# Two recurrence heads at a time: interleaved levels and pairwise tails in a hybrid decoder layer

## What is computed

```
b = jnp.cumsum(gc, axis=2)
diff = jnp.where(causal, b[:, :, :, None, :] - b[:, :, None, :, :], -jnp.inf)
att = jnp.einsum('bhtk,bhsk,bhtsk->bhts', qc, kc, jnp.exp(diff))
out = jnp.einsum('bhtk,bhkv->bhtv', qc * jnp.exp(b), S) + jnp.einsum('bhts,bhsv->bhtv', att, vc)
S = jnp.exp(b_last[:, :, 0, :])[..., None] * S + jnp.einsum('bhsk,bhsv->bhkv', kc * jnp.exp(b_last - b), vc)
```

## Time and profile before

| | |
|---|---|
| median of three runs | 1977.64 us (1977.2 to 1979.1) |
| profiled execution | 1976.55 us |
| its span | 1974.6 us |
| TensorE busy, share of the span | 1724.5 us, 87% |
| VectorE busy | 803.4 us, 41% |
| ScalarE busy | 432.9 us, 22% |
| GpSimd busy | 542.7 us, 27% |
| mean granted TensorE clock | 0.918 |

### The profile page before, as it was taken

The page is one execution under the profiler, slowest core; times in us unless marked ns, Lnnn a source line. Parts: engine busy times, 40 slices in busy tenths (PEclk is TensorE's granted clock), DMA queues, the critical chain, the costliest instruction groups (busy, mean ns, idle before and its releaser), DMA issues.

```text
span 1974.6 us, 28840 instructions
## 1 busy us (share of the span) xinstructions
PE 1724.5 (87%) x12863; PEld 1577.7 (80%) x12863; DVE 803.4 (41%) x1160; ACT 432.9 (22%) x576; POOL 542.7 (27%) x202
## 2 busy tenths in 40 slices
PE   2899999998797799877599978776688899999997
PEld 1799999998765799866388755554687899999997
DVE  4412111135217599866576654221465412111121
ACT  2311111112133123200123333221122211111111
POOL 0233343334312123300011122332122233333331
PEclk9999999999688899966599989887799999999999
DMA  4132233223311122201132137887512122333222
GB/s 136 43 86 73 74 101 86 79 69 117 121 48 34 55 89 86 75 23 44 51 115 67 68 126 284 316 303 299 207 64 86 49 80 73 89 90 82 79 74 78
DMA packets 191499, 203.43 MB, mean 103 GB/s; under 512 B 7104, under 2 KB 176832, under 8 KB 182928
## 3 DMA queue, kind: packets, MB, share of 16 engines
q1 hardware_dynamic: 172336, 105.56, 18.7%
q0 software_dynamic: 11680, 75.57, 10.5%
q10 hardware_dynamic: 7360, 20.47, 2.7%
HBM read 187.21 MB, written 14.30 MB: 102 GB/s over the span
## 4 chain that ended last, share of the span: by engine, by line
PE 75%; DVE 12%; DMA 6%; ACT 3%; issue 3%; SPq 0%; POOL 0%; ACTq 0%; DVEq 0%
PE ps L1291 21%; PE ps L1292 20%; PE ps L1293 20%; DMA k_page<-in_cache_k,kv_row 3%; DMA v_page<-in_cache_v,kv_row 2%; PE ps L1638 2%; PE ps L1591 1%; PE ps L1609 1%; DVE att L1033 1%; PE ps L1714 1%; DVE m_hi L1233 1%; DVE nf L841 1%; DVE n_lo L844 1%; ACT n_hi L515 1%; PE ps L1653 1%
## 5 line engine op out<-in xcount | busy, mean ns | idle before, releaser
L411 POOL TENSOR_TENSOR w_lo<-raw,w_hi 128x2048 fp32r<-128x2048 f32 (+1 forms) x108 | 456.7, 4229 | 1071.9 <-ACT w_hi L500 1071.9
L1291 PE MATMUL ps<-n_lo,w_hi 128*128 128x288 f32 x1856 | 557.6, 300 | 26.7 <-DVE n_lo L844 17.5
L1292 PE MATMUL ps<-n_hi,w_lo 128*128 128x288 f32 x1856 | 551.1, 297 | 0.0
L1293 PE MATMUL ps<-n_hi,w_hi 128*128 128x288 f32 x1856 | 549.3, 296 | 0.0
L1291 PEld LDWEIGHTS ps<-n_lo,w_hi 128*128 128x128 f32 x1856 | 351.6, 189 | 44.6 <-issue 28.7
L1293 PEld LDWEIGHTS ps<-n_hi,w_hi 128*128 128x128 f32 x1856 | 352.9, 190 | 0.0
L1292 PEld LDWEIGHTS ps<-n_hi,w_lo 128*128 128x128 f32 x1856 | 352.1, 190 | 0.0
L500 ACT ACTIVATE w_hi<-raw 128x2048 fp32r<-128x2048 f32 (+1 forms) x108 | 187.9, 1740 | 287.9 <-PE ps L1293 279.6
L856 DVE TENSOR_TENSOR hf<-sg,ps 128x576 f32<-128x576 f32 x44 | 33.2, 754 | 449.6 <-ACT sg L526 449.6
L1292 PE MATMUL ps<-hid_hi,w_lo 128*128 128x288 f32 x704 | 207.7, 295 | 0.0
L1293 PE MATMUL ps<-hid_hi,w_hi 128*128 128x288 f32 x704 | 207.5, 295 | 0.0
(11 more groups left out here) (256 smaller groups left out, 2317.1 us busy)
## 6 DMA issues: line engine op xcount, KB each, us to landing
raw<-in_w_in SPq DMA_DIRECT2D x23, 1024.0 KB, 5.3
raw<-in_ffn_w_gate SPq DMA_DIRECT2D x44, 512.0 KB, 4.0
raw<-in_ffn_w_up SPq DMA_DIRECT2D x44, 512.0 KB, 5.3
raw<-in_ffn_w_down SPq DMA_DIRECT2D x32, 704.0 KB, 4.5
scratch_g<-g_out ACTq DMA_DIRECT2D x8, 576.0 KB, 2.8
gates<-scratch_g ACTq DMA_DIRECT2D x4, 1152.0 KB, 8.8
raw<-in_w_out SPq DMA_DIRECT2D x4, 1024.0 KB, 4.9
scratch_x<-xT ACTq DMA_DIRECT2D x1, 2304.0 KB, 12.6
```

What stands on the lines that cost most here:

```text
L411: pool.tensor_tensor(w_lo[:, u % NRAW, :n], raw[:, u % NRAW, :n], w_hi[:, u % NW, :n].bitcast(F32), ALU.subtract).then_inc(S("w_lo_done"), 1)
L1291: pe.matmul(dst, hi, x_lo, start=first, stop=False)
L1292: pe.matmul(dst, lo, x_hi, start=False, stop=False)
L1293: return pe.matmul(dst, hi, x_hi, start=False, stop=last)
```

## The change

Heads are handled in groups of two, heads(g) for g = 0, 1. In the level loop each engine does level L of head a = 0, then of head a = 1, and goes on to the next level. Each head of the group has its own part of left, q_lev, k_lev, att, att_s, k_rows, state, state_s and v_own, and its own banks: 4 + a and 6 + a. There is one q_lev and k_lev buffer and one bank per head instead of two by level parity: VectorE waits for the products of level L-1 before it writes the operands of level L, and TensorE waits until level L-1 is copied out. The semaphores of the levels and the transfers exist once per a.

The tails follow pairwise: final operands of both heads, transposes of both, k_rows of both, v_own of both, then on TensorE the whole chain of the first head and that of the second; on VectorE the state updates of both, then state_s of both. The output of the second head goes to banks 4 and 6, and its v_own products to banks 2 and 3. TensorE waits for state_s_done and o_out once per group. GpSimd loads the states of two heads at the start, and each further one when the store of its buffer has landed. v_own moves to other memory, which is free there.

The lines that are removed stand in the functions above. The core of the diff:

```diff
@@ -248,15 +248,16 @@
         key, e = sb("key", [P, HB, T], at=e)
         query, e = sb("query", [P, HB, T], at=e)
         out_gate, e = sb("out_gate", [P, 4, T], at=e)
-        left, e = sb("left", [P, T], at=e)
+        left, e = sb("left", [P, 2, T], at=e)
         q_lev, e = sb("q_lev", [P, 2, T], at=e)
         k_lev, e = sb("k_lev", [P, 2, T], at=e)
-        att, e = sb("att", [P, 4, P], at=e)
-        att_s, e = sb("att_s", [NS, NS], at=e)
-        k_rows, e = sb("k_rows", [P, NT, KD], at=e)
-        state, e = sb("state", [P, 2, VD], at=e)
-        state_s, e = sb("state_s", [P, NB, VD], at=e)
-        v_own, e = sb("v_own", [NS, NB, VD], at=e)
+        att, e = sb("att", [P, 2, 4, P], at=e)
+        att_s, e = sb("att_s", [NS, 2, NS], at=e)
+        k_rows, e = sb("k_rows", [P, 2, NT, KD], at=e)
+        state, e = sb("state", [P, 2, 2, VD], at=e)
+        state_s, e = sb("state_s", [P, 2, NB, VD], at=e)
+        v_own, e = sb("v_own", [NS, 2, NB, VD], at=bias_at - 4 * (256 + 384 + 512))
+        assert e <= bias_p_at
 
...
+            def state_load(h):
+
+                if h < 2:
 
                     pool.wait_ge(S("index_done"), 1)
-                pool.dma_start(state_s[:, :, :], w["state_hgrn"][:, h].rearrange("b k v -> k b v")).then_inc(S("state_in"), 16)
+                else:
+                    pool.wait_ge(S(f"state_s_out{h % 2}"), 16)
+                pool.dma_start(state_s[:, h % 2, :, :], w["state_hgrn"][:, h].rearrange("b k v -> k b v")).then_inc(S(f"state_in{h % 2}"), 16)
+
+            def state_store(h):
                 pool.wait_ge(S("state_s_done"), h + 1)
-                pool.dma_start(out[9][0, :, h].rearrange("b k v -> k b v"), state_s[:, :, :]).then_inc(S("state_s_out"), 16)
-                pool.wait_ge(S("state_s_out"), 16 * (h + 1))
+                pool.dma_start(out[9][0, :, h].rearrange("b k v -> k b v"), state_s[:, h % 2, :, :]).then_inc(S(f"state_s_out{h % 2}"), 16)
 
...
+            state_load(0)
+            state_load(1)
+            for h in range(2):
+                state_store(h)
+                state_load(h + 2)
+            state_store(2)
+            state_store(3)
...
+            def heads(g):
+                for a in range(2):
+                    act.wait_ge(S("k_turned"), 2 * g + a + 1)
+                    act.activation(k_rows[:, a, 1:NT, :], ps[:, 4 + a, :].rearrange("p (t k) -> p t k", t=4), ACT.Copy)
+                    act.activation(k_rows[0:NS, a, 0, :], ps[0:NS, 6 + a, 0:KD], ACT.Copy).then_inc(S("k_rows_done"), 1)
+                for a in range(2):
+                    h = 2 * g + a
+                    act.wait_ge(S("o_summed"), h + 1)
+                    act.activation(oT[:, h, NS:T], ps[:, 4 * a, :], ACT.Copy)
+                    act.activation(oT[:, h, 0:NS], ps[:, 1 + 5 * a, 0:NS], ACT.Copy).then_inc(S("o_out"), 1)
+                    act.wait_ge(S("state_done"), 4 * h + 4)
+                    act.dma_start(out[5][0, 0, h], state[:, a, 1, :]).then_inc(S(f"state_out{a}"), 16)
...
+                    for a in range(2):
+                        h = 2 * g + a
+                        if L > 1:
+                            dve.wait_ge(S(f"level_done{a}"), 8 * g + L)
+                        dec, q, k = (level_view(x[:, h, :], L) for x in (decay, query, key))
+                        into_q, into_k = (level_view(x[:, a, :], L) for x in (q_lev, k_lev))
+                        dve.tensor_tensor(into_q[:, :, 1, :], q[:, :, 1, :], dec[:, :, 1, :], ALU.mult)
+                        if L == 1:
+                            dve.memset(left[:, a, :], 1.0)
+                            dve.tensor_copy(into_k[:, :, 0, :], k[:, :, 0, :]).then_inc(S(f"level_in{a}"), 1)
+                        else:
+                            dve.tensor_tensor(into_k[:, :, 0, :], k[:, :, 0, :], level_view(left[:, a, :], L)[:, :, 0, :],
+                                              ALU.mult).then_inc(S(f"level_in{a}"), 1)
+                        end, mid, first, right = level_views(h, L)
+                        dve.wait_ge(S(f"level_in{a}"), 8 * g + L)
+                        link(dve.tensor_tensor(first, first, end, ALU.mult))
+                        link(dve.tensor_tensor(right, right, mid, ALU.mult))
+                        level_out(a, L - 1)
+
+                for a in range(2):
+                    h = 2 * g + a
+                    dve.wait_ge(S(f"level_done{a}"), 8 * g + 8)
+                    dve.tensor_tensor(q_lev[:, a, :], query[:, h, :], decay[:, h, :], ALU.mult)
+                    dve.tensor_tensor(k_lev[:, a, :], key[:, h, :], left[:, a, :], ALU.mult).then_inc(S(f"level_in{a}"), 1)
+                    level_out(a, 7)
+                for a in range(2):
...
+                for a in range(2):
+                    h = 2 * g + a
+                    dec = decay[:, h, :]
+                    for i in range(4):
+                        dve.wait_ge(S("state_added"), 4 * h + i + 1)
...
+                for a in range(2):
+                    h = 2 * g + a
+                    dve.wait_ge(S("o_summed"), h + 1)
+                    link(dve.tensor_tensor(state_s[:, a, :, :], state_s[:, a, :, :],
+                                           decay[:, h, NQ - 1:NS:NQ].unsqueeze(2).to_broadcast([P, NB, VD]), ALU.mult))
+                    dve.wait_ge(S("head_read"), h + 1)
+                    for m in range(2):
+                        part = state_s[:, a, 4 * m:4 * m + 4, :]
+                        ins = dve.tensor_tensor(part, part, ps[:, 2 + m if a else 5 + 2 * m, :].rearrange("p (b v) -> p b v", b=4),
+                                                ALU.add)
+                    ins.then_inc(S("state_s_done"), 1)
...
+            def heads(g):
+                if g == 0:
...
+                    pe.wait_ge(S("o_out"), 2)
+                    pe.wait_ge(S("state_s_done"), 2)
                 for L in range(len(LEVELS)):
...
+                    for a in range(2):
+                        h = 2 * g + a
+                        if L:
+                            pe.wait_ge(S(f"level_in{a}"), 8 * g + L)
+                            pe.wait_ge(S(f"level_out{a}"), 8 * g + L)
+                        q = q_lev[:, a, :] if L else query[:, h, :]
+                        k = k_lev[:, a, :] if L else key[:, h, :]
+                        if LEVELS[L] < NQ:
+                            pe.matmul(ps[0:NS, 6 + a, 0:NS], k[:, 0:NS], q[:, 0:NS], start=True, stop=True)
+                        for t in range(1, NT):
+                            ins = pe.matmul(ps[:, 4 + a, P * (t - 1):P * t], k[:, cols(t)], q[:, cols(t)],
+                                            start=True, stop=True)
+                        ins.then_inc(S(f"level_done{a}"), 1)
+                for a in range(2):
+                    pe.wait_ge(S(f"level_in{a}"), 8 * g + 8)
+                    pe.wait_ge(S(f"level_out{a}"), 8 * g + 8)
+                    for t in range(NT):
+                        dst = ps[0:NS, 6 + a, 0:KD] if t == 0 else ps[:, 4 + a, P * (t - 1):P * t]
+                        ins = pe.transpose(dst, k_lev[:, a, cols(t)], ident)
+                    ins.then_inc(S("k_turned"), 1)
+                for a in range(2):
+                    h = 2 * g + a
+                    o_p, o_s = ps[:, 4 * a, :], ps[:, 1 + 5 * a, 0:NS]
+                    pe.wait_ge(S("k_rows_done"), h + 1)
+                    v = [stage[0:rows(t), g, t, a * VD:(a + 1) * VD] for t in range(NT)]
+                    for i in range(4):
+                        if 4 * h + i >= 2:
+                            pe.wait_ge(S("state_done"), 4 * h + i - 1)
+                        pe.matmul(ps[:, 2 + i % 2, 0:VD], k_rows[:, a, i + 1, :], v[i + 1], start=True,
+                                  stop=True).then_inc(S("state_added"), 1)
+                        pe.matmul(o_p[:, P * i:P * i + P], v[i + 1], att[:, a, i, :], start=True, stop=i == 0)
...
+                    pe.wait_ge(S("v_own_done"), h + 1)
+                    pe.wait_ge(S("k_rows_done"), 2 * g + 2)
+                    if a:
+                        pe.wait_ge(S("state_done"), 4 * h + 4)
+                    for m in range(2):
+                        ins = pe.matmul(ps[:, 2 + m if a else 5 + 2 * m, :], k_rows[0:NS, a, 0, :],
+                                        v_own[:, a, 4 * m:4 * m + 4, :], start=True, stop=True)
+                    ins.then_inc(S("head_read"), 1)
```

199 lines of the change are left out of this document (63 added, 136 removed).

## The result

| | before | after |
|---|---|---|
| median (range), runs of this comparison | 1978.37 us (1977.2 to 1980.81), 4 | 1961.07 us (1957.67 to 1964.96), 4 |
| ratio (95% interval) | | 0.9912 (0.989 to 0.9933) |
| profiled execution | 1976.55 us | 1957.67 us |
| its span | 1974.6 us | 1955.9 us |
| mean granted TensorE clock | 0.918 | 0.926 |

It is faster, by 17.3 us in the medians and 18.9 us in the two profiled executions. The forecast was 10.6 us less (1977.64 to 1967); 1961.07 lies inside the range of 1958 to 1974, near its low end.

What follows compares the result with a forecast made beforehand. VectorE was taken to bound the level loops, TensorE, with holes, the tails. Tail structure 9.1 us plus chains 2.9 less late groups 2.0 gave 10.0 us gained, so 1967 us; range 1958 to 1974.

Steps and rivals of the forecast that it cites:

- Tails' structure, 9.1 us: Tails: first head's transposes hidden, 2.8 us; k_rows copies hidden, 3.4 us; first head's state_s additions hidden, 2.9 us.
- the 2.9 us item: Tails: the first head's state_s additions run during the second head's chain; 1.45 us gone per pair, 2.9 us.
- Levels, 0 us of gain and 2.0 us of late groups: Level loops: VectorE sets the pace, so interleaving gains nothing; the tighter handshake with TensorE costs 1.0 us per pair.
- 0.15 us late at each of some five groups: Small levels at the low clock: TensorE's loop takes 2.73 us against VectorE's 2.58; 0.8 us per pair.
- 0.7 at the start of a pair: Pair start: TensorE runs three low-clock rounds, 7.5 us, before VectorE's third group, ready after two; 0.7 us more.
- Rival 4: Level loops: interleaving also fills VectorE's small gaps, 3.6 us at most, no late groups; 15.6 us gained, 1962; chance 0.06.
- rival 3: Level loops: handshake longer than the rows show, 28 groups each 0.25 us late; 5 us gained, 1972.5; chance 0.12.
- v_own, the loads of states and the GpSimd collision, 0 us: Two v_own hidden at the low clock, state loads early enough, 4.30 us vector product under GpSimd's subtraction unchanged; 0 us.
- The chains and the clock, 2.9 us: TensorE's product chains in the four tails: 9.95 us each, 39.8 us instead of 42.7; 2.9 us gone.
- The bound of 28.4 us: Tails: lower bound for the four chains, all at the high clock, 7.1 us each.
- Rival 1: Tails: chains run at the high clock, 28.4 us in all; 21 us gained, 1956.5; chance 0.15.
- Rival 2: Tails: all four chains stay at the low clock, 51.6 us; 2.8 us slower, 1980.4; chance 0.05.

Runs made afterwards that it cites:

- serial_tails: The changed kernel with levels interleaved, but the second head's tail begun only when the first head's state_s is done; 1975.08 us, ratio 0.9994 to before.
- state_between: The changed kernel, but the second chain of a pair waits until state_s of the first head is done; 1968.49 us, ratio 0.9952 to before.
- late_turn: The changed kernel with the second head's transposes put back behind the first head's products with state_s; 1964.63 us, ratio 0.9963 to before.
- seq_levels: The changed kernel with level loops one head after the other, two buffers and banks each, tails still pairwise; 1960.31 us, ratio 0.991 to before.
- fill_after: The changed kernel with five unread 288-column products behind the products of each of the last four levels; 1952.86 us, ratio 0.9912 to before.
- wide_first: The changed kernel with the first head's two wide v_own products ahead of its att_s and state_s products; 1949.5 us, ratio 0.9884 to before.
- before_again: The kernel before, unaltered, profiled a second time; 1970.22 us in one run, stage 135.8 us, chains 39.8 us.
- the first group: The runs of after_again, seq_levels, serial_tails and state_between, beside which the kernel before had a median of 1976.96 us (17 runs).
- after_again: The changed kernel, unaltered, run once more; 1963.93 us, ratio 0.9925 to before, stage 122.2 us, chains 34.6 us.
- fill_before: The kernel before with five unread 288-column products behind the products of each of the last four levels; 1964.03 us, ratio 0.9958 to before.

## Why the prediction was right, and where it was off

- *Tails' structure, 9.1 us.* Held: 9.2 in the two profiles. Each item has a row: the first head's transposes at 863.36, no k_rows wait on TensorE, one hole of 1.5 us between the pairs. serial_tails, which undoes all three, gives back 10.5 us and the whole gain in time; state_between gives back 2.3 us of the 2.9 us item; late_turn 3.6 us with that of the transposes and copies.
- *Levels, 0 us of gain and 2.0 us of late groups.* The sign held, the size was too large: the loops grew by 0.6 us in all, and are 1.5 longer than those of seq_levels. VectorE waited 0.8 us for TensorE before q_lev products (1.4 with the mask copy), under the 3 us that would have refuted it. The terms "0.15 us late at each of some five groups" and 0.7 at the start of a pair took all small levels to run at the low clock. Rival 4 (interleaving fills VectorE's gaps) falls with seq_levels, rival 3 (a long handshake) with the same rows.
- *v_own, the loads of states and the GpSimd collision, 0 us.* Held: the first state copy came before it was needed, TensorE never waited for state_in, and the 4.30 us moved to head 1. That v_own would cost 0.7 us at the high clock, fill_after and wide_first show as 0.74.
- *The chains and the clock, 2.9 us.* This is the mis-sized term: 8.7 us in the two profiles (8.1 by the lengths in the table). The failing step is "I take the value of the three like ones, 9.95 us, for all four": it had no place for a clock that differs from tail to tail. Two of the four, those of the first pair, took 7.8 and 6.9 us; the second pair's took 9.9 and 10.0, as assumed. I said the clock would be wrong if the four chains added up far from 40 us; they add up to 34. The bound of 28.4 us was itself read a little too high: it took 2.45 us for the wide products from a chain in which the clock fell in them, where 1.91 is their time at the high clock, and a whole chain at it takes 6.87 us. Part of the 8.7 (3.0 us) is head 2 of the kernel before, which its second profile does not have; so against before_again the chains give 39.8 - 34.6 = 5.2 us and the rest of the stage (the levels in it) 96.0 - 87.4 = 8.6, together 13.8 us, beside 13.0 us in the medians of the first group. That the time lay inside the range owes something to luck: the sum had 10.0 us where the stage gave 17.3, the term of the clock was three times as large as said, and the range reached that far for the sake of rivals 1 and 4.
- *Rival 1, chains at the high clock.* Half true: nearly right for the first pair (7.8 and 6.9 us), wrong for the second, in which TensorE was busy 20.60 of 20.70 us and its clock averaged 0.67. The Trainium skill says in "TensorE: Matmul & The Clock Gate" (Part 1: The HAM clock gate) that activity releases the throttle. The trace agrees in that the clock rose in the first chain of each pair; it stayed up through the first pair and fell again twice in the second, with TensorE busy.
- *Rival 2, the low clock stays.* No chain of after did so. A whole low chain (12.9 us) was seen in the kernel before, late_turn and wide_first, one each, so the case was real; but never in all four.
- *What would show it.* The loops 43.0 and 40.3 us (said 40 to 41), output_norm at 943.85 (said near 952): the 8 us between are the chains, 5.7 below what was said, the late groups, 1.4 below, and the 1.1 us by which the stage began sooner.

What stays open: why the clock stays up through one tail and falls in the next of the same code. The pattern was the same in both profiles of after, differed between two of before, and moved with each edit. So the structure of the tails is shown as the cause of some 9 us; that the chains are shorter is measured, why they are is not shown. No run tells apart what went before the tail from what is in it.

## What to carry to other kernels

When short stages of two independent items alternate with long ones, pair the short ones: each item's hand-offs then run under the other's products, and holes that stand in every item's tail go at once. Interleaving the long stages is a separate decision; where one engine already fills them, it only trades double buffers for a tighter handshake. Experiments that undo one of the two parts each tell which of them pays; here one paid for all.

Removing all holes went with shorter chains too. Where each chain follows a wait (before, before_again, serial_tails) none of the twelve took under 9.85 us; with pairwise tails half of those of after and after_again took 6.87 to 7.85. How much of that another kernel would get can't be read from one execution. Before sizing such a term, look whether an odd stretch (head 2's tail here) repeats in a second profile.

## What the runs showed that was not expected

- In all but one of the chains in which the clock fell, it fell in or behind sixteen instructions of 8 columns, with TensorE busy through them: 0.22 us a product before them, 3.60 us for the wide products behind them where 1.92 is the high-clock time. Lifting the clock before them (head 0 of fill_before) doesn't prevent it, putting the wide products first (wide_first) moved it into them and the next chain in one pair, and no fall came in the other. Whether the narrow products cause it is not shown.
- sample_attention takes 218 to 233 us for the same instructions and bytes, at 276 to 289 GB/s in the two profiles above. That scatter is nearly as large as the whole effect measured here.
